# Gate and up weights in blocks of 1 MB in place of 2 MB from the seventh round of experts on

## The reference, cut to what matters

```python
def swiglu(x, w_gate, w_up, w_down):
    return (jax.nn.silu(x @ w_gate) * (x @ w_up)) @ w_down
...
    _, eidx = lax.top_k(sel, TOP_K)            # 6 of 64 experts for each token
...
    def run(args):
        xe, e = args
        return swiglu(xe, w_gate[e], w_up[e], w_down[e])
```

## Time and profile before

| | |
|---|---|
| time, median of 3 runs | 1316.24 us (1315.61 to 1318.78) |
| profiled execution: its own time | 1320.9 us |
| profiled execution: span | 1319.1 us |
| TensorE matmuls busy | 1222.7 us (93%) |
| VectorE, ScalarE busy | 280.5 us (21%), 239.5 us (18%) |
| read from HBM | 493.73 MB |
| mean granted TensorE clock | 0.971 |

### The profile page before, as it was taken

One profiled execution on the slowest core, in us unless ns is written; L12 is line 12 of the kernel. 1 busy time (PEld: TensorE's weight loads), 2 busy tenths in 40 slices (PEclk: granted clock), 3 DMA queues, 4 the chain that ended last, 5 costly groups with the idle time before them and its releaser, 6 DMA issues.

```text
span 1319.1 us, 25797 instructions
## 1 busy us (share of the span) xinstructions
PE 1222.7 (93%) x11196; PEld 838.6 (64%) x11196; DVE 280.5 (21%) x720; ACT 239.5 (18%) x534; POOL 2.8 (0%) x13
## 2 busy tenths in 40 slices
PE   6999999999998898889899999999999898988897
PEld 4566587676765565656565658866767565656664
DVE  1252353101011010111034525511111010101012
ACT  2363122101010110011034521411001101000102
POOL 0000000000000000000000000000000000000000
PEclk9999999999998898899899999999999999999989
DMA  9879839999999999999966753999999999999994
GB/s 398 334 314 354 345 134 424 420 425 424 424 426 424 428 426 426 428 422 420 419 284 237 264 214 154 410 420 424 423 427 424 424 426 426 429 424 427 418 420 182
DMA packets 54115, 496.96 MB, mean 377 GB/s; under 512 B 9104, under 2 KB 9360, under 8 KB 12048
## 3 DMA queue, kind: packets, MB, share of 16 engines
q1 hardware_dynamic: 49968, 493.75, 90.0%
q10 hardware_dynamic: 4064, 2.00, 0.5%
HBM read 493.73 MB, written 2.00 MB: 376 GB/s over the span
## 4 chain that ended last, share of the span: by engine, by line
PE 57%; DMA 35%; DVE 3%; SPq 2%; issue 1%; ACT 1%; DVEq 0%
DMA gu<-in_exp_w_both 32%; PE PS L2259 18%; PE PS L1759 7%; PE PS L2182 5%; PE PS L2091 4%; PE PS L2297 4%; PE PS L2189 4%; PE PS L1701 2%; DMA arena<-in_exp_w_both 2%; PE PS L1669 1%; SPq L632 1%; PE PS L2140 1%; DMA gu<-in_w_in_wide 1%; PE PS L1882 1%; PE PS L1893 1%
## 5 line engine op out<-in xcount | busy, mean ns | idle before, releaser
L2259 PE MATMUL PS<-gu,arena 128*32 128x256 f32 (+1 forms) x4000 | 339.1, 407 | 66.6 <-DMA gu<-in_exp_w_both 46.1
L2259 PEld LDWEIGHTS PS<-gu,arena 128*32 128x32 f32 (+1 forms) x4000 | 196.4, 119 | 212.3 <-issue 83.4
L2182 PE MATMUL PS<-arena 128*128 128x128 f32 x1408 | 176.3, 278 | 0.5 <-ACT arena L1091 0.5
L2182 PEld LDWEIGHTS PS<-arena 128*128 128x128 f32 x1408 | 164.0, 192 | 18.3 <-issue 17.2
L2259 PE MATMUL PS<-arena 128*32 128x256 f32 (+1 forms) x768 | 175.4, 387 | 0.0
L2297 PE MATMUL PS<-dn,arena 128*32 128x512 f32 (+1 forms) x976 | 160.1, 595 | 1.6 <-DVE arena L1578 1.6
L2189 PE MATMUL PS<-arena 128*128 128x256 f32 x704 | 160.2, 380 | 0.0
L2297 PE MATMUL PS<-arena 128*32 128x512 f32 (+1 forms) x368 | 152.1, 595 | 0.0
L2189 PEld LDWEIGHTS PS<-arena 128*128 128x128 f32 x704 | 130.2, 190 | 19.1 <-issue 3.3
L1584 DVE TENSOR_TENSOR arena<-arena,PS 128x256 f32<-128x256 f32 x44 | 18.5, 421 | 546.6 <-ACT arena L1087 546.6
L2259 PE MATMUL PS<-xh,arena 128*32 128x256 f32 x608 | 133.3, 389 | 0.0
(11 more groups left out here) (265 smaller groups left out, 1022.0 us busy)
## 6 DMA issues: line engine op xcount, KB each, us to landing
gu<-in_exp_w_both SPq DMA_DIRECT2D x64, 2048.0 KB, 25.4
dn<-in_exp_w_down SPq DMA_DIRECT2D x80, 1024.0 KB, 24.1
gu<-in_exp_w_both SPq DMA_DIRECT2D x44, 1024.0 KB, 15.1
arena<-in_exp_w_down SPq DMA_DIRECT2D x42, 1024.0 KB, 24.7
gu<-in_w_ada_pieces SPq DMA_DIRECT2D x20, 2048.0 KB, 9.1
arena<-in_exp_w_both SPq DMA_DIRECT2D x18, 2048.0 KB, 23.8
xh<-in_exp_w_both SPq DMA_DIRECT2D x12, 2048.0 KB, 34.1
gu<-in_w_in_wide SPq DMA_DIRECT2D x8, 2048.0 KB, 14.5
```

Of the source, the lines that this page charges most:

```text
L2182: ins = mmul(PS[:, 4, (c % 4) * P:(c % 4) * P + P], h_tok[:, g, c], onehot[b][:, g], start=(g == 0), stop=(g == 1))
L2259: ins = mmul(PS[w * h:w * h + w, 5, FF * half:FF * half + FF], xg[:, k, w * h:w * h + w], weights[half][:, k], start=(k == 0), stop=(k == ...
```

## The change

Rounds 6 to 16 load their gates and then their ups with `load_halves_to`, and TensorE waits for the ups of these rounds by themselves. `UPS` now has every round from 6 to 19; its counts in the loop rise by 48 each turn (three loads of 16). What the loads wait for and the buffers they go to stay the same.

```diff
-UPS = {0: 48, 1: 48, 2: 80, TRIOS - 3: 96, TRIOS - 2: 128, TRIOS - 1: 144}
-EVEN_UPS, ODD_UPS = 128, 144
+UPS = {0: 48, 1: 48, 2: 80}
+UPS.update({r: 32 * (1 - r % 2) + 48 + 48 * ((r - UNROLLED) // 2 + 1) for r in range(UNROLLED, TRIOS)})
+EVEN_UPS, ODD_UPS = UPS[TRIOS - 2], UPS[TRIOS - 1]
...
                 sp.wait_ge(S["up_done"], r0 + 7)
-                load_to(6, (A, B, D_), x6)
+                for half in range(2):
+                    load_halves_to(6, (A, B, D_), x6, half)
...
-                trio_loads(0, UNROLLED + 1, this)
+                trio_loads(0, UNROLLED + 1, this, split=True)
                 with sp.Fori(0, (TRIOS - UNROLLED - LAST) // 2 - 1) as m:
                     for r in (UNROLLED + 2, UNROLLED + 3):
-                        trio_loads(m, r, lambda x: bass.ds(m * 8 + x, 1))
+                        trio_loads(m, r, lambda x: bass.ds(m * 8 + x, 1), split=True)
...
                     if r in UPS:
-                        ups = [(S[f"{name}_up_in"], UPS[r] + ups_of[odd])]
+                        ups = [(S[f"{name}_up_in"], m * 48 + (UPS[r] + ups_of[odd]))]
```

## The result

The changed kernel takes 1320.25 us (median of 7 runs, 1319.95 to 1325.4) against 1315.16 us (7 runs, 1313.59 to 1318.78). The ratio is 1.0052, 95% interval 1.0040 to 1.0063: 0.5% slower, 5.3 to 8.3 us by the interval and 5.1 us by the medians. The middle of the interval is 6.8 us; it lies above the medians because three of the seven runs of the changed kernel stand apart, at 1323.9 to 1325.4. The forecast was 6.8 us slower, 1323.0 us.

The account below looks back on a forecast made before the run. The prediction took DMA to bound both expert streams. Issues, the added wait and earlier release counted 0, the slower rate 6.8 us, passed on whole; on the median 1316.24 this gave 1323.0 us, range 1317.5 to 1328.

Parts of the forecast that it names:

- The bound: Both expert streams: DMA share 1.01 at 426 GB/s, a round as long as its bytes, 22.15 us; TensorE has slack.
- Issues, the added wait and the earlier release: Rounds 6 to 16: 132 issues for 66, a second wait per round, buffers free about 3.5 us earlier; cost and gain 0.
- The rate: Rounds 6 to 16 of each layer: 1 MB blocks move at 420 GB/s, not 426; 6.8 us slower in all.
- the rival that the lower rate belongs to something else: Rounds 6 to 16: the lower rate mostly does not appear; no measurable change, chance 0.19 together with the clock.
- the second reading: The rate's cost from the chain's starts: split pairs 0.55 us longer than unsplit, 6.1 us; layers alone 12.0 and 0.2.
- The lateness passes whole: End of each layer: TensorE waits for round 18's ups, so the stream's 3.4 us per layer is not absorbed.
- The sum: Whole kernel: 6.8 us added to the profiled span, 1325.9 us; on the median 1316.24, 1323.0 us, +0.5%.
- the forecast's own case: Whole kernel slower by the rate, within 1320.5 to 1328 us; chance 0.72.
- The loop of latency: Expert loop: 33 us from issue to landing belongs to the transfer; 45 us faster, 1271 us; chance 0.06.
- A transfer that pays its own start: 66 more transfers at 2.3 us each: 150 us slower, 1470 us; chance 0.03, together with a starving queue.
- The clock: Round 18's up matmuls: shorter waits keep the clock up, saving up to 5.8 us, 1317.3 us; within the 0.19 for no change.

Follow-up runs that it names:

- the two variants beside it: The changed kernel with gate and up in turn and one wait for both, 1321.21 us; the changed kernel with split rounds' gates issued on "gate_done", 1320.5 us.

## Why the prediction was right

**The bound** was read rightly. Both streams are bound by DMA: SyncE's waits for TensorE nearly vanish with the change and no time comes back, and in the run without the separate wait none is lost. One reading was short: the 14 waits of 46.1 us are those for blocks in the tensor gu alone; there are 9 more for xh (18.7 us) and 2 for arena (1.8 us), 66.6 us in all. The longest is still 4.8, and the argument stands.

**Issues, the added wait and the earlier release** were costed at 0. SyncE stands in its issues in all rounds (14.55 us for six) and the DMA share doesn't move from 1.01. The first wait, for the gates, is gone in the loop, and the second, for the ups, is 2.9 us in mean (13.4 and 12.3 us in 9 waits from 380 to 588 us), not "some 4".

**The rate** was the step that carried the sum. Its mechanism held in this form: the loads of the split rounds move more slowly. Two things in it were less than exact. The size: 0.32 us a round came from the split rounds at the end, 420 GB/s; in the loop the rate is 422, 9.437 / 0.422 - 9.437 / 0.426 = 0.21 us a round, 4.6 us in all and 4.7 by the distances, in place of 6.8. The last rounds are slower by 1 or 2 GB/s even when nothing in them is split (424 and 425), so a third or so of the difference between 426 and 420 did not belong to the split; the rival that the lower rate belongs to something else had that much of it right. And the name: I wrote "block size", but the runs show that it is the row of one partition, 8 KB in place of 16 KB, and that the 1 MB of a DMA doesn't matter. The packets say the same: one of 16 KB took 616 ns before and two of 8 KB 627. Of the second reading, layer 0's 12.0 us and layer 1's 0.2 us came from one pair of starts each, too few to size the term; their mean, 6.1, was nearer to it than either.

**The lateness passes whole.** It did: TensorE waits 3.7 us for layer 1's round 18 ups after the change as well, and both layers end later. I had 3.4 us a layer and it is 2.3 and 2.4.

**The sum.** 1323.0 is 2.75 us above the measured median. 1.7 of that is the term of the rate against the medians' 5.1, and 1.1 the start: with seven runs the median before is 1315.16 and not 1316.24. The band for the forecast's own case, 1320.5 to 1328, misses the measured 1320.25 by a hair; the range of 1317.5 to 1328 holds it. That the middle of the ratio's interval is 6.8 us is luck, as the term that gave 6.8 was too large.

**The rivals.** The loop of latency falls, as SyncE's waits for TensorE went from 58.7 to 3.3 us and the stream lost 4 GB/s in place of gaining. A transfer that pays its own start falls with 1 MB blocks at 426 GB/s. The clock gave back a little against the profiled execution before: the 64 matmuls behind round 18's wait took 5.35 us in both layers, in place of 6.09 and 6.58. That is 2.0 us of the 5.8 that this rival could have had.

**What stays open.** Against the profiled execution before, the streams account for 4.7 us. The kernel with every other partition costs nothing and is a second yardstick: its first expert matmuls start at 206.40 and 840.49 us and round 18's ups at 629.17 and 1264.54, distances of 422.77 and 424.05. Against these the kernel after the change is 2.7 and 2.55 us longer, 5.2 together. The medians differ by 5.1, so they leave nothing to place; the two variants beside it are 6.0 and 5.8 us above their medians of before, and the ratio allows up to 8.3. Half a microsecond or more may be outside the streams, and the runs do not tell. Nor is it shown why rounds 17 and 18 move a little more slowly than the loop: 420 against 422 GB/s when both are split, 424 and 425 against 426 when neither is.

## What to carry to other kernels

Where a window shows the DMA engines busy without a gap, expect little of a finer wait on the data (here it was worth nothing that could be measured), and ask what the finer load does to the rate: look at the bytes that lie together for one partition, the row, not at the size of the DMA. Where the stream ends and compute stands behind the last landings, the same split can pay (here some 11 us). A chain that alternates between a long DMA and its issue can stand in a full queue, too, where it looks like latency; bytes over time and the DMA share tell the two apart. And when an edit is meant to move an issue, look in the trace whether the issue moved.

## What the runs showed of the hardware

The rate in a saturated stream by the length of a row, with a third of the bytes in 8 KB rows throughout: 426 GB/s with 16 KB, 422 with 8 KB, 414 with 4 KB.

A load into 64 neighbouring partitions moved at about half the rate (235 GB/s in the stream, of which a third was in full-width loads), while all DMA engines showed as busy; into every other partition it moved at the full 426. The Trainium skill (SBUF — State Buffer, section "Door 1: The DMA port swizzle (why `[64,N]` ≈ `[32,N]`)") has the rule: partitions 0 to 63 reach only 8 of 16 ports, by a bit of the partition's number that every other partition does not fix. The two runs agree with it.

What fills the queue seems to be rows as well, and not DMAs or bytes. With 1 MB blocks in rows of 8 KB (128 rows each) six issues took 14.55 us; with as many 1 MB blocks in rows of 16 KB on every other partition (64 rows each) they went through in 3.82 us:

```profile
461.42 3.82 SPq L728 DMA_DIRECT2D gu<-in_exp_w_both  x6
```

Three whole loads of 2 MB in rows of 16 KB (128 rows each) took 1.37 us; the same three in rows of 8 KB (256 rows each) stood for 9.11 us:

```profile
463.74 9.11 SPq L636 DMA_DIRECT2D gu<-in_exp_w_both  x3
```

These are single rounds, and how many rows the queue holds is not worked out here.
